# One residual subtraction and one rounding copy of a weight block change places around a triangular inversion

## The reference, cut to what matters

```python
xx = jnp.pad(h, ((0, 0), (1, 0), (0, 0)))[:, :-1] - h
xs = h[None] + xx[None] * mu[:, None, None, :]
rkv = jnp.einsum('pbtd,pde->pbte', xs[:3], w_rkv)      # receptance, keys, values
...
y = _wkv7_scan(r_h, heads(decay), k_h, v_h, kk, kk * heads(a))   # 256 dependent steps
```

## Time and profile before

| | us |
|---|---|
| median of 3 runs | 1059.74 (1058.86 to 1060.34) |
| the profiled execution, its own time | 1059.96 |
| its span on the core | 1058.2 |
| PE busy in the span | 1038.6 (98%) |
| DVE busy | 713.5 (67%) |
| ACT busy | 539.4 (51%) |
| POOL busy | 32.5 (3%) |
| granted PE clock, mean | 0.998 |

### The profile page before, as it was taken

How to read it: one execution, slowest core, us unless ns; L and a number is a source line. 1 busy time by engine, 2 the same in 40 slices (tenths; PEclk the granted TensorE clock), 3 DMA queues, 4 the chain that set the end, 5 groups by cost and what they waited for, 6 DMA issues and landing times.

```text
span 1058.2 us, 21160 instructions
## 1 busy us (share of the span) xinstructions
PE 1038.6 (98%) x8984; PEld 1008.7 (95%) x8984; DVE 713.5 (67%) x994; ACT 539.4 (51%) x651; POOL 32.5 (3%) x39
## 2 busy tenths in 40 slices
PE   7999999999999999999999999999999999999997
PEld 7899999999997899999999999999898999999997
DVE  6789674455567787665565657899978666555464
ACT  6947654444347465345344445897543254443431
POOL 0004000000000000000000000042000000000000
PEclk9999999999999999999999999999999999999999
DMA  9622475555754745556555554414200157555511
GB/s 294 212 88 81 159 242 196 169 188 182 294 159 125 233 160 199 160 165 233 164 195 165 192 197 121 140 59 152 71 2 2 54 181 254 189 182 175 198 40 41
DMA packets 119043, 167.02 MB, mean 158 GB/s; under 512 B 5825, under 2 KB 99649, under 8 KB 118593
## 3 DMA queue, kind: packets, MB, share of 16 engines
q1 hardware_dynamic: 117792, 165.92, 48.2%
q10 hardware_dynamic: 1184, 0.17, 0.1%
HBM read 165.03 MB, written 1.05 MB: 157 GB/s over the span
## 4 chain that ended last, share of the span: by engine, by line
PE 83%; DVE 9%; ACT 4%; issue 2%; DMA 1%; SPq 1%; DVEq 0%; ACTq 0%
PE banks L2081 24%; PE banks L2083 24%; PE banks L2082 24%; DVE sb_w_low L1246 1%; DVE sb_arena L1914 1%; DVE sb_state L1911 1%; DMA sb_raw<-in_w_in 1%; PE banks L2666 1%; ACT sb_w_high L659 1%; SPq L537 1%; PE banks L2533 1%; PE banks L2777 0%; DVE sb_arena L1405 0%; DVE sb_state L1402 0%; PE banks L2836 0%
## 5 line engine op out<-in xcount | busy, mean ns | idle before, releaser
L1246 DVE TENSOR_TENSOR sb_w_low<-sb_raw,sb_w_high 128x2048 fp32r<-128x2048 f32 x148 | 338.0, 2289 | 243.6 <-ACT sb_w_high L659 243.5
L659 ACT ACTIVATE sb_w_high<-sb_raw 128x2048 fp32r<-128x2048 f32 x148 | 281.9, 1911 | 264.6 <-PE banks L2083 261.6
L2081 PE MATMUL banks<-sb_act_high,sb_w_low 128*128 128x256 f32 x1352 | 386.4, 286 | 1.1 <-DVE sb_arena L1787 0.7
L2083 PE MATMUL banks<-sb_act_high,sb_w_high 128*128 128x256 f32 x1352 | 381.9, 282 | 0.0
L2082 PE MATMUL banks<-sb_act_low,sb_w_high 128*128 128x256 f32 x1352 | 380.1, 281 | 0.0
L2081 PEld LDWEIGHTS banks<-sb_act_high,sb_w_low 128*128 128x128 f32 x1352 | 254.6, 188 | 3.3 <-DVE sb_arena L1787 0.9
L2082 PEld LDWEIGHTS banks<-sb_act_low,sb_w_high 128*128 128x128 f32 x1352 | 255.9, 189 | 0.5 <-issue 0.2
L2081 PE MATMUL banks<-sb_hidden_high,sb_w_low 128*128 128x256 f32 x896 | 253.7, 283 | 0.6 <-DVE sb_hidden_low L1725 0.6
L2083 PEld LDWEIGHTS banks<-sb_act_high,sb_w_high 128*128 128x128 f32 x1352 | 253.4, 187 | 0.0
L2083 PE MATMUL banks<-sb_hidden_high,sb_w_high 128*128 128x256 f32 x896 | 253.4, 283 | 0.0
L2082 PE MATMUL banks<-sb_hidden_low,sb_w_high 128*128 128x256 f32 x896 | 251.9, 281 | 0.0
(11 more groups left out here) (443 smaller groups left out, 1048.9 us busy)
## 6 DMA issues: line engine op xcount, KB each, us to landing
sb_raw<-in_ffn_w SPq DMA_DIRECT2D x64, 1024.0 KB, 5.2
sb_raw<-in_w_up SPq DMA_DIRECT2D x16, 1024.0 KB, 5.4
sb_raw<-in_w_down SPq DMA_DIRECT2D x16, 1024.0 KB, 5.0
sb_raw<-in_sgu_w_in SPq DMA_DIRECT2D x16, 1024.0 KB, 5.4
sb_raw<-in_rwkv_w_rkv SPq DMA_DIRECT2D x12, 1024.0 KB, 5.1
sb_raw<-in_w_in SPq DMA_DIRECT2D x8, 1024.0 KB, 10.1
sb_raw<-in_sgu_w_out SPq DMA_DIRECT2D x8, 1024.0 KB, 5.0
sb_raw<-in_w_out SPq DMA_DIRECT2D x4, 1024.0 KB, 5.2
```

The costliest lines, as they stand in the source:

```text
L659: nc.scalar.activation(whi[s][:], raw[s][:], ACT.Copy).then_inc(hi_done, 1)
L1246: nc.vector.tensor_tensor(wlo[s][:], raw[s][:], f32(whi[s][:]), ALU.subtract).then_inc(lo_done, 1)
L2081: nc.tensor.matmul(dst, l_lo, r_hi, start=start, stop=False, **kw)
L2083: return nc.tensor.matmul(dst, l_hi, r_hi, start=False, stop=stop, **kw)
```

## The change

Two places are edited, with the same instructions as before. On DVE `low` of unit 10 stands ahead of step j = 1 in place of j = 8. On ACT `high` of unit 10 stands behind the fifth of the eight `mixed_high(2, k)` in place of behind the eighth; `high` of unit 11 stays behind all of them. No instruction, wait or transfer is added or taken away.

```diff
-    BASE_LOWS = {8: U_RKV + 10, 15: U_RKV + 11}
+    BASE_LOWS = {1: U_RKV + 10, 15: U_RKV + 11}
...
             diagonals(2)
             diagonals(3)
-            for k in range(KT):
+            for k in range(5):
                 mixed_high(2, k, RW.XS)
+
             high(U_RKV + 10)
+            for k in range(5, KT):
+                mixed_high(2, k, RW.XS)
             high(U_RKV + 11)
```

## The result

| | before | after |
|---|---|---|
| median of 20 runs, us | 1059.61 (1058.34 to 1060.34) | 1060.43 (1059.40 to 1063.39) |
| ratio after to before | | 1.0014, 95% interval 1.0008 to 1.0020 |
| the profiled execution | 1059.96 (span 1058.2) | 1062.21 (span 1060.4) |

The change makes the kernel slower by 0.14%, about 1.5 us, which twenty runs tell from no change (the two medians are 0.82 us apart). The median hides how. The 20 times after lie in groups: ten from 1059.40 to 1060.05, two at 1060.8, and eight from 1061.89 to 1063.39, where the 20 times before have none. The profiled execution is one of the eight. The groups differ in the granted clock of PE, too: its mean over the execution is 0.996 or 0.997 in all eight, and 0.998 or 0.999 in eleven of the other twelve (the twelfth is 1060.85, with 0.997).

A forecast was written before the change was run, and what follows sets the result against it. PE sets the time nearly everywhere, but DVE's substitution bounds this stretch. DVE 0, PE's lateness 1.67 less slack 1.33 gave +0.3 us: 1060.3 for a profiled execution, 1060.0 as median; range 1058.3 to 1061.0.

The forecast's parts named there:

- DVE gains nothing: DVE's substitution: held off by POOL five times as before, its chain stays as long, ± 0.1 us.
- PE's slack at the joining: Before right_products: packed, PE could begin it at 762.15 but begins at 763.48, so 1.33 us of lateness cost nothing.
- Who waits for POOL: PE's pass over the low activations: POOL's tile 7 comes at 734.45, PE uses it at 732.78; PE stands 1.67 us later.
- S = 1.67: PE's lateness in us from its wait for POOL's low activations, carried through units 9 to 11; bounds 0 and 1.9.
- S - 1.33: At the joining: PE's lateness less its slack, if positive, moves what follows; 1.67 - 1.33 = +0.3 us.
- POOL not held off: Faster rival: POOL runs through low of unit 10, DVE saves three turns, 1.3 us: 1058.4; chance 0.22.
- POOL doesn't get its turn: Slower rival: after the low, POOL waits until the receptance piece ahead of step 6; +2.8 us, 1062.6; chance 0.07.
- The late high part: Rival on ACT: it slips over 0.3 us and PE's first pass waits, swallowed by the POOL wait: 1060.0; chance 0.02.
- The move does nothing: Rival: PE's wait for POOL is shorter than its slack at the joining, both ends cancel: 1059.7; chance 0.14.

The follow-up runs named there:

- `low` ahead of step 4: The kernel before with low of unit 10 ahead of step 4 in place of step 8, ACT's order unchanged: 1062.06 us, ratio 1.0019.
- the receptance first: The changed kernel with the last piece of the receptance ahead of step 1, before the moved low, in place of step 6: 1058.93 us, ratio 0.9994.
- the filled wait: The changed kernel with three dummy matmuls on PE ahead of unit 9, where it waits: 1060.74 us, ratio 1.0009.
- the receptance ahead of step 9: The kernel before with the last piece of the receptance ahead of step 9 in place of step 6: 1064.43 us, ratio 1.0041.
- the DVE half alone: The kernel before with low of unit 10 ahead of step 1, its high part still behind the eighth mixed_high: 1064.05 us, ratio 1.0040.

## Why the prediction was wrong

**What held.** DVE and POOL take turns, and the `low` holds POOL off: 2.79 us for one POOL instruction (forecast 2.9), 2.74 for the `low` (2.7 to 2.8). The last POOL instruction ends at 734.16 in the times of before (forecast 734.35), though the profile shows only 0.61 us of idle time of PE for it and not 1.7. ACT's three late `mixed_high` made nobody wait. DVE gains nothing: from low of unit 9 to line 2000 it is 37.75 us against 37.56, 0.19 longer, a little outside the forecast's ± 0.1. PE's slack at the joining was put at 1.33 and is 1.26 in the changed kernel, and 1.27 with `low` ahead of step 4 (2.22 - 0.95). On one detail the prediction weighed its rows against the Trainium skill ("SBUF — State Buffer", Who interferes with whom: whoever issues first has the shared ports for its whole instruction), and here the trace agrees with the skill. The product of step 1 takes 0.75 us at 730.06, so POOL, whose instruction had been issued at 727.94, went ahead of it; and the end of unit 8 is late by 1.52 us (730.61 to 734.21 is 3.60, before 2.08), nearer to the 1.53 of that rule than to the 1.67 that the sum took.

**The step that failed: "Who waits for POOL", with S = 1.67 for PE's lateness.** S isn't made by POOL. The prediction had units 9 to 11 follow unit 8 back to back, and took POOL for the only thing that PE waits for. It counted the moved `low` against what stands behind it in the substitution, and named the piece of the receptance only in a rival, as a gap for POOL. It didn't ask who waits for that piece, though the move sets 2.2 us of work in front of it and unit 9 was waiting 0.72 us for it already. The sum should have had S = 2.2 or so from there. POOL's 1.5 us of lateness lie inside it, of which 0.72 were a wait anyway. So by POOL alone unit 9 would be some 0.8 to 0.95 us late (1.53 or 1.67 less 0.72), under the slack of 1.33, and the sum 0; the run with the receptance first measures 0.64 and shows that it costs nothing. With S = 2.30 the prediction's own formula, S - 1.33, gives +1.0: that is what the filled wait measures at `right_products` (+1.02), and near what lies between the groups at full clock (0.83, from the medians of the lower groups, nine runs each: 1059.50 against 1058.67).

**What the prediction didn't have: the clock.** It priced PE's wait as a wait. In the profiled execution PE was idle for 0.30, 0.31 and 1.49 us in a row; the clock fell 0.4 us into the last of them, and 5.7 us of work at 1.2 GHz followed, 2.51 us more. None of it met slack, since the 1.26 were used up. Eight runs of twenty show it as a group of their own. The forecast of +0.3 was thus some 0.7 us short where the clock was kept, and some 3 us short in the eight. That the range held the median, 1060.43, is luck: it lies between two groups. And the chance of 0.89 for "within 0.2%" rested on cases of which none was the right one.

**The rivals.** POOL not held off: wrong (2.79 us). POOL doesn't get its turn: wrong, it did after every step. The late high part: wrong. "The move does nothing": true for what POOL does to PE, but not for the move.

**What stays open**: why the clock falls in some executions and not in others of the same kernel (a single wait of 2.94 us kept it in the profiled execution with `low` ahead of step 4, and seven of its twelve executions lost it), why it falls 0.4 us into the wait in one trace (the changed kernel) and only near the end of 5.26 us in another (the receptance ahead of step 9), and why it stays low for 6.8 us in the first and 3.4 us in the second. Whether PE's two short waits for POOL make the loss more frequent in the full change was not tested; alone, with the receptance first, they lost it in none of eleven executions.

## What to carry to other kernels

Before an instruction is moved up a queue, write down every instruction that it passes, and look up in the trace who waits for each of them: the one that frees a PSUM bank is short, belongs to other work and is easily read over. A wait that is already in the profile, even a hidden one of 0.7 us, marks the instruction past which nothing should be moved. And a wait of PE is worth more than its length where it may cost the clock; filling it with dummy matmuls took the upper group of times away, though not the wait.

## What the runs showed of the hardware

- The price of a PE wait depended on the clock: with the clock kept, 1.0 us for a unit 9 that is 2.2 to 2.3 us late; 2.51 us more where the granted clock was 0.50 for the first 5.7 us behind the wait (the changed kernel), and 1.3 and 1.5 us more in the two other traces that lost it (the receptance ahead of step 9, the DVE half alone). Three dummy matmuls (1.46 us) in a wait of 1.5 us kept it at 1.00, in the trace, and no run of eleven was in the upper group.
- A POOL instruction that had asked for its turn during a 2.74 us subtraction of two SBUF operands on DVE got it ahead of the next DVE instruction, although that one had no wait in front of it: 0.75 us for 60 elements where it is 0.22 with POOL idle.
- A DVE instruction with one operand in PSUM (the piece of the receptance, 128x512) takes 0.69 us among POOL's low activations as well as after them.
- The work up to the inversion shifts as a whole between executions: low of unit 9 starts between 722.99 and 724.72 us in the ten traces that leave the work ahead of it as it was. Between the profiles of before and after the 1.34 us come from the landing of the first weights. The times of several kernels lie in two groups with the clock kept, as the 20 before do (nine up to 1059.06, eleven from 1059.53); that this shift makes them is likely and not shown.
